# Scores of heads 4 to 7 behind the gates' products, ahead of the second Y unit, on one Trainium2 core

## The reference

```
xr = causal_depthwise_conv(xr, conv_w, conv_b)            # 4 taps
r = sigmoid(xr_heads @ w_a + b_a); i = sigmoid(xr_heads @ w_i + b_i)
a = exp(-8 * r * softplus(-lambda)); u = sqrt(1 - a*a) * (i * xr)
y_lru = scan(h = a*h + u) * gelu(yg)
q, k = rms_norm per head
s = q @ k.T / 8 - slope_h * distance, causal;  y_attn = softmax(s) @ v
x = x + concat(rms_norm(y_lru), rms_norm(y_attn)) @ w_out
up = causal_depthwise_conv(rms_norm(x) @ w_up, ...)       # 3 taps
x = x + (gelu(gate) * val) @ w_down                       # d_ff 2816
```

## Time and profile before

| | us |
|---|---|
| median of 3 runs | 290.94 (290.81 to 291.02) |
| the profiled execution | 290.89 |
| its span, first to last instruction | 289.1 |
| TensorE products busy (PE) | 284.2, 98% |
| TensorE weight loads busy (PEld) | 246.5, 85% |
| VectorE (DVE) | 244.1, 84% |
| ScalarE (ACT) | 201.7, 70% |
| GpSimd (POOL) | 11.4, 4% |

### The profile page before, as it was taken

One profiled execution on the slowest core, in us unless ns is written; L12 is line 12 of the kernel. 1 busy time (PEld: TensorE's weight loads), 2 busy tenths in 40 slices (PEclk: granted clock), 3 DMA queues, 4 the chain that ended last, 5 costly groups with the idle time before them and its releaser, 6 DMA issues.

```text
span 289.1 us, 5011 instructions
## 1 busy us (share of the span) xinstructions
PE 284.2 (98%) x1646; PEld 246.5 (85%) x1646; DVE 244.1 (84%) x448; ACT 201.7 (70%) x380; POOL 11.4 (4%) x26
## 2 busy tenths in 40 slices
PE   7999999999999999999999999999999999999996
PEld 7688999898788999888888888888888888888885
DVE  2998898889999787999988888888888888888865
ACT  4793599999895685877776766667666666676540
POOL 3000005600000000000000000000000000000000
DMA  7999950340375714475657474454637454200004
GB/s 284 426 422 416 390 190 0 147 145 11 136 252 186 244 49 151 142 290 156 281 161 279 145 248 173 158 170 150 264 145 290 145 172 175 88 0 0 0 0 145
DMA packets 8111, 52.23 MB, mean 181 GB/s; under 512 B 928, under 2 KB 1312, under 8 KB 2080
## 3 DMA queue, kind: packets, MB, share of 16 engines
q1 hardware_dynamic: 7920, 51.50, 48.4%
q0 software_dynamic: 176, 0.53, 0.5%
HBM read 50.98 MB, written 1.05 MB: 180 GB/s over the span
## 4 chain that ended last, share of the span: by engine, by line
PE 95%; DMA 2%; ACT 1%; SPq 0%; DVE 0%; issue 0%
PE bank L1408 25%; PE bank L1052 15%; PE bank L1053 14%; PE bank L1056 14%; PE bank L1412 13%; PE bank L1108 3%; PE bank L1361 3%; DMA x_tok<-in_x_dram 2%; PE bank L1372 1%; PE bank L1172 1%; PE bank L1296 1%; PE bank L1203 1%; PE bank L1212 1%; PE bank L1330 1%; PE bank L1166 1%; ACT ygate L392 0%
## 5 line engine op out<-in xcount | busy, mean ns | idle before, releaser
L693 DVE TENSOR_TENSOR w_lo<-raw,w_hi 128x1024 fp32r<-128x1024 f32 x93 | 110.9, 1220 | 4.6 <-ACT w_hi L380 4.0
L380 ACT ACTIVATE w_hi<-raw 128x1024 fp32r<-128x1024 f32 x83 | 84.3, 1060 | 3.1 <-PE bank L1056 2.7
L1408 PE MATMUL bank<-h_both,w_hi 128*128 128x512 f32 x320 | 79.7, 391 | 0.1
L1408 PEld LDWEIGHTS bank<-h_both,w_hi 128*128 128x128 f32 x320 | 58.7, 188 | 11.6 <-issue 0.3
L1412 PEld LDWEIGHTS bank<-h_both,w_lo 128*128 128x128 f32 x320 | 43.7, 190 | 3.1
L1412 PE MATMUL bank<-h_both,w_lo 128*128 128x256 f32 x320 | 44.6, 282 | 0.0
L607 ACT ACTIVATE tanh_a<-bank 128x256 f32<-128x256 f32 x44 | 16.8, 381 | 38.7 <-PE bank L1412 38.3
L1052 PE MATMUL bank<-w_hi,act_hi 128*128 128x512 f32 (+1 forms) x90 | 34.9, 388 | 0.0
L1053 PE MATMUL bank<-w_lo,act_hi 128*128 128x512 f32 (+1 forms) x90 | 34.8, 387 | 0.0
L1056 PE MATMUL bank<-w_hi,act_lo 128*128 128x512 f32 (+1 forms) x90 | 34.6, 384 | 0.0
L975 DVE TENSOR_TENSOR ygate<-bank,tanh_a 128x256 f32<-128x256 f32 x44 | 18.5, 420 | 12.4 <-ACT tanh_a L607 12.3
(11 more groups left out here) (190 smaller groups left out, 409.1 us busy)
## 6 DMA issues: line engine op xcount, KB each, us to landing
raw<-in_stream_dram SPq DMA_DIRECT2D x47, 1024.0 KB, 4.8
x_tok<-in_x_dram SPq DMA_DIRECT2D x2, 512.0 KB, 5.0
out_dram<-x_tok SPq DMA_DIRECT2D x3, 256.0 KB, 2.1
p_T<-in_gates_dram POOLq DMA_DIRECT2D x1, 512.0 KB, 9.9
out_dram<-x_tok SPq DMA_DIRECT2D x2, 128.0 KB, 2.0
par<-in_params_dram SPq DMA_DIRECT2D x1, 117.0 KB, 6.6
mix_g<-in_params_dram POOLq DMA_DIRECT2D x1, 4.0 KB, 5.5
```

The costliest lines, as they stand in the source:

```text
L380: act.activation(hi_tile(u)[:, :], raw_unit(u), ACT.Copy).then_inc(hi_done, 1)
L693: dve.tensor_tensor(w_lo[u % RING][:, :], raw_unit(u), hi_tile(u)[:, :].bitcast(F32), ALU.subtract).then_inc(lo_done, 1)
L1408: pe.matmul(acc[:, :], whi[:, kc, :], h_both[:, kc, :, :].rearrange("p b t -> p (b t)"), start=kc == 0, stop=False)
```

## The change

Scores 4 to 7 are issued directly behind the gates' products. Behind them stands a wait for `gates_read` at 2, then Y1 and Y2. Scores 4 and 5 keep banks 0 and 1; head 6 goes to bank 3, head 7's two parts to free columns of banks 1 and 2. So that Y0 does not share what they use, Y0 and Y3 are in bank 2, Y1 and Y2 in bank 4, and V in banks 5 and 3. The waits follow: scores 6 and 7 wait for four shifts, the shift of head 5 for all scores, transposes 2 and 3 for five and eight shifts, the first gelu for three Y units (it now takes chunks 1 and 2, the second chunks 0 and 3).

```diff
-        Y_ACC, V_ACC = bank[2:4], bank[4:6]
+        Y_ACC = (bank[2][:, 0:SEQ], bank[4][:, 0:SEQ], bank[4][:, SEQ:2 * SEQ], bank[2][:, SEQ:2 * SEQ])
+        Y_PAIRS = ((slice(1, 3), bank[4], U_Y + 3), (slice(0, 4, 3), bank[2], U_Y + 4))
+        V_ACC = (bank[5], bank[3])
...
-        S_BANK, P_BANK = (*bank[0:4], *bank[0:2], *bank[4:6]), (*bank[6:8], *bank[0:2])
+        P_BANK = (*bank[6:8], *bank[0:2])
...
+        def s_at(h, m):
+
+            at = KEY_AT[m]
+            if h == 7:
+                at = (SCORES, SEQ)[m]
+            s_bank = bank[h % 4] if h < 6 else (bank[3] if h == 6 else bank[1 + m])
+            return s_bank[:, at:at + KEYS[m]]
...
             for j in range(2):
-                act.wait_ge(unit_used, U_Y + 2 * j + 2)
-                act.activation(ygate[:, 2 * j:2 * j + 2, :], Y_ACC[j][:, :].rearrange("p (c t) -> p c t", c=2),
+                chunks, acc, units = Y_PAIRS[j]
+                act.wait_ge(unit_used, units)
+                act.activation(ygate[:, chunks, :], acc[:, :].rearrange("p (c t) -> p c t", c=2),
                                ACT.Gelu_apprx_tanh).then_inc(ygate_done, 1)
...
             def shift(h):
-                dve.wait_ge(scores, h + 1)
+                dve.wait_ge(scores, HEADS if h == 5 else h + 1)
...
-                    ins = dve.tensor_tensor_reduce(probs[h][:, part], S_BANK[h][:, part],
+                    ins = dve.tensor_tensor_reduce(probs[h][:, part], s_at(h, m),
...
                 elif h == 6:
-                    pe.wait_ge(gates_read, 2)
+                    pe.wait_ge(shifted, 4)
...
                 if h == 2:
-                    pe.wait_ge(shifted, 6)
+                    pe.wait_ge(shifted, 5)
+                if h == 3:
+                    pe.wait_ge(shifted, HEADS)
...
             for c in GATE_ORDER:
                 gates_product(c)
-            y_unit(1)
             score_pair(4)
             score_pair(6)
+            pe.wait_ge(gates_read, 2)
+            y_unit(1)
             y_unit(2)
```

More of the change, by code:

```diff
@@ L1171, in score_part @@
                 c, rows_h = h // 2, slice(HEAD_DIM * (h % 2), HEAD_DIM * (h % 2 + 1))
-                return pe.matmul(S_BANK[h][:, KEY_AT[m]:KEY_AT[m] + KEYS[m]],
+                return pe.matmul(s_at(h, m),
                                  q_T[rows_h, c, P * m:P * (m + 1)], k_T[rows_h, c, 0:KEYS[m]],
@@ L1216, in y_unit @@
             def y_unit(c):
-                cols_unit(U_Y + c, Y_ACC[c // 2][:, SEQ * (c % 2):SEQ * (c % 2 + 1)])
+                cols_unit(U_Y + c, Y_ACC[c])
             pe.wait_ge(hi_done, hi_count(U_K))
```

## The result

The changed kernel takes 292.15 us (median of 7 runs, 291.96 to 292.30) against 290.94 before: a ratio of 1.0042, 95% interval 1.0033 to 1.0052. It is slower by 1.2 us. The forecast was 292.2. (One of the seven runs of before stood at 404.58 us and is left out of the ratio.) The profiled executions of the two kernels are 1.33 us apart (292.22 and 290.89).

The account below looks back on a forecast made before the run. TensorE's back-to-back queue was taken to bound the kernel: 1.46 us of wait less 0.19 of saved seams gave about +1.28 on the profiled 290.89, so 292.2 us, range 291.7 to 292.8.

Parts of the forecast that it names:

- What bounds the kernel: TensorE's queue, back to back from 20 us on: each 1 us of added wait lengthens the kernel by 1 us.
- The sum of +1.28: Transposes 0 to 3 on TensorE start at 59.92 instead of 58.64 us, the whole predicted loss.
- The wait: TensorE before Y1 idles some 1.5 us until ScalarE's sixth gate reading ends at 54.01; Y1 starts at 54.06.
- 0.05 us for the release: Delay from the end of ScalarE's sixth reading to Y1's start on TensorE; uncertain from 0 to 0.1 us.
- Y1 and Y2: TensorE behind the wait: Y1 takes 2.98 us with a first step of 0.22, Y2 takes 2.88.
- The seams: Extra time at TensorE's product shape changes; one fewer each way with gates and scores adjacent, a gain of 0.19 us.
- Shifts, exponentials, DMA at nothing: Moved work on VectorE, ScalarE and DMA queues was costed at 0, as no further TensorE wait follows.
- rival 3: ScalarE's pause at 59.2 makes a late exponential or gelu stop TensorE again: 0.5 us more, 292.7 us; 6%.
- 1: No wait before Y1: the gates are read by 52.6 us and only seams count, 290.7 us; 2%.
- 2: The wait before Y1 is partly given back later, at most 0.4 us, 291.8 us; 4%.
- 4, the falling clock: The pause before Y1 brings TensorE's clock to the low level for Y1: 3.0 us more, 295.2 us; 4%.
- the upper bound of Y1's first step: Y1's first step on TensorE after the idle stretch: at most 0.22 plus 0.39 us for a slow product.

Follow-up runs that it names:

- r_first: The changed kernel with ScalarE reading the first gates of chunks 0 and 2 first, Y1 waiting for those two readings alone; 290.74 us, 0.9993 of before.
- late_16: The changed kernel with ScalarE's rounding of unit 16 moved behind the gates' readings, VectorE's split of it behind the gates' input product; 291.50 us.
- wait_four: The changed kernel with Y1 waiting for all four chunks' gate readings instead of two; 296.61 us, ratio 1.0195 to before.

## Why the prediction was right

*What bounds the kernel.* Right: with 1.29 us lost at 59.93, the last product starts at 287.44 instead of 286.12, 1.32 later. Nothing was given back later; TensorE's idle time from 60 to 280 us is 0.07, as before 0.08. The sum of +1.28 stands between the 1.21 by which the medians differ and the 1.33 of the profiled executions; that 292.2 met 292.15 more closely than the runs agree with each other (291.96 to 292.30) is luck.

*The wait.* The step that carries the sum. Release at 54.02, predicted 54.01; Y1 at 54.08, predicted 54.06. The 0.05 us for the release measured 0.06. r_first (no wait: 1.41 us less) and late_16 (an earlier reading: 0.65 less, with Y1 0.53 earlier) show that ScalarE's reading is the cause and not something that merely stands beside it.

*Y1 and Y2.* First step 0.22, then 0.12: 54.08 to 57.05 is 2.97 (predicted 2.98), Y2 2.88 (2.88). The weights were not loaded during the wait: the weight load stood idle for 1.79 us and started at 54.07, with the product. But the 0.22 is not a price of the wait. In r_first, where nothing is waited for, the first load also starts only with its product (52.66 and 52.67), and the step is 0.22 as well. It belongs to the change of product shape:

```profile
54.07 0.19 PEld L1063 LDWEIGHTS bank<-h_both,w_hi 128*128 128x128 f32 x1 [1.79 <-ACT gate_i L520]
```
```profile
52.66 0.19 PEld L1068 LDWEIGHTS bank<-h_both,w_hi 128*128 128x128 f32 x1 [0.33 <-issue]
```

By the rule of the Trainium skill that I weighed there (TensorE: Matmul & The Clock Gate, "Step-by-step: what each phase is for"), loads are pulled ahead of products in flight. The traces agree inside a unit, where a load starts about 0.12 us ahead of its product (54.18 and 54.30 for Y1's second), and show no such lead at the first step behind 64-row products, with a wait or without one.

*The seams.* The seam between gates and scores, left open between free and full, costs what gates to a Y unit cost (49.22 to 51.10 is 1.88, against 1.89). In the changed kernel this lies under the wait. In r_first it does not, and there 0.19 us for one seam each way fits the medians (290.93 or 290.98 against 290.74) and the 0.18 in the rows.

*Shifts, exponentials, DMA at nothing.* VectorE's shift of head 4 started at 54.61 (predicted 54.7), and its lead of 0.35 us at 56.98 vanished in its idle time at 65.45. ScalarE paused 1.23 at head 0's eviction (predicted about 1.28), and that pause set no second wait of TensorE: rival 3 did not occur.

*Rivals.* 1 and 2 are excluded by the wait's row and by the 1.32 us that are still there at the last product. 4, the falling clock, did not occur in the changed kernel: steps of 0.12 behind the pause, at a granted clock (behind the five busy times) of 1.00:

```profile
54.00:57.00 3.00, 2.92 (x24) 2.93 (x25) 2.83 (x21) 2.84 (x7) 0.96 (x2) 1.00 0.20 76
```

But my 4% for it had poor support. I took a pause of 0.56 us as evidence, which was the weight load's; the products themselves had paused for 0.12 (10.70 to 10.82). Twice the pause of the changed kernel (2.86 us) is enough for the fall, and it costs 1.5 us, not the 3.0 that I had set as its price. The margin between this kernel and one of 293.7 us or more was less than 1.5 us of waiting.

I also misread. The 0.79 at 8.74 is no sign of the low level. It stands at 0.79 or 0.80 in the trace of every kernel here, always in the first product behind four records of unsplit float32 products (line 1102 before, 1113 after), and in the changed kernel the stretch around it (8 to 10 us) has a granted clock of 1.00:

```profile
7.65 1.96 PE L1113 MATMUL bank<-raw,xc 128*128 128x512 f32 x4 [0.34 <-ACT xc L420]
9.04 0.80 PE L1095 MATMUL bank<-w_hi,h_both 128*128 128x512 f32 x1
9.67 0.39 PE L1097 MATMUL bank<-w_lo,h_both 128*128 128x512 f32 x1
```

So the 0.39 in the upper bound of Y1's first step had no slow product behind it. It did no harm, since that step took 0.22. What a slow product looks like, wait_four shows: 0.41 us instead of 0.28 for 256 columns, and steps of 0.213 instead of 0.12.

## What to carry to other kernels

Where one engine's queue is full to the end, read an added wait as two timestamps: when the queue arrives at it, and when its releaser ends; the difference goes to the end one for one, as long as the clock holds (here up to a pause of 1.4 us). Moving short work ahead of long work in such a queue is only free if what the long work covered is still covered: here Y1 had hidden ScalarE's table load and readings. When a wait is for a bank, ask which of its readers really touch the bank and put those first; here two readings of six were enough, and the wait was gone.

## What the runs showed of the hardware

A pause of TensorE of 1.4 us left its clock alone (12 runs, granted clock 0.999 or 1.0), pauses of 2.9 and 4.3 us did not. The fall came late: after the pause products ran at the full rate for about 1 us, and only then at half the clock, for about 3.4 us in both kernels, while TensorE was busy. So the longer pauses cost their own length and 1.5 us more here, once about 2.6, and the loss stands in the rows behind the resumption, where no wait is listed. The Trainium skill (TensorE: Matmul & The Clock Gate, "HAM oscillation — how this bites in real kernels") tells of a TensorE that is throttled back in a long wait and whose next products start cold. The fall is in these runs too, but not the cold start: eight products in wait_four came at the full rate first. Where between 1.4 and 2.9 us of pause the step lies was not tried.
